# First projection unit of a hybrid attention and RWKV-7 block cut into three column parts

## What is computed

```python
h = jnp.concatenate([meta, x], axis=1)               # 528 x 1024
u = rms_norm(h, norm_mix_pre[l]) @ w_in[l]           # 528 x 5376
u_sb, u_rw, gate_sb, gate_rw = jnp.split(u, cut, axis=-1)
o_sb = stick_breaking_attention(sq, sk, sv)
o_rw = rwkv7_time_mix(...)
merged = sigmoid(gate_sb) * (o_sb @ w_branch_sb) + sigmoid(gate_rw) * (o_rw @ w_branch_rw)
h = h + rms_norm(merged @ w_out[l], norm_mix_post[l])
f = (silu(f @ w_ffn_gate) * (f @ w_ffn_up)) @ w_ffn_down    # f = rms_norm(h)
h = h + rms_norm(f, norm_ffn_post[l])
```

## Time and profile before

| | |
|---|---|
| median of 3 runs | 890.42 us (890.24 to 892.93) |
| the profiled execution, its own time | 892.45 us |
| its span, first to last instruction | 890.6 us |
| busy: PE / PEld | 98% / 81% |
| busy: DVE / ACT / POOL | 55% / 46% / 10% |
| the chain that ended last: PE / DVE / issue, ACT | 93% / 5% / 1% each |
| moved by the transfers | 82.82 MB, 93 GB/s over the span |

### The profile page before, as it was taken

How to read it: one execution, slowest core, us unless ns; L and a number is a source line. 1 busy time by engine, 2 the same in 40 slices (tenths; PEclk the granted TensorE clock), 3 DMA queues, 4 the chain that set the end, 5 groups by cost and what they waited for, 6 DMA issues and landing times.

```text
span 890.6 us, 19075 instructions
## 1 busy us (share of the span) xinstructions
PE 874.9 (98%) x8261; PEld 724.3 (81%) x8261; DVE 487.5 (55%) x644; ACT 412.6 (46%) x573; POOL 92.4 (10%) x92
## 2 busy tenths in 40 slices
PE   6999999999999999999999999999999999999997
PEld 5999999867787777767888898888888888888886
DVE  5459997346767656639575754444444444422333
ACT  6444666359788765555343642222222222211331
POOL 2015543111010101041100000000000000000000
PEclk9999999999999999999999999999999999999999
DMA  9322223311201121142267323333333333333321
GB/s 276 101 83 85 71 72 96 119 50 38 73 4 39 39 74 38 38 131 72 87 221 269 85 67 100 94 94 94 94 94 94 94 94 94 95 96 96 103 85 71
DMA packets 109008, 82.82 MB, mean 93 GB/s; under 512 B 2895, under 2 KB 99449, under 8 KB 108682
## 3 DMA queue, kind: packets, MB, share of 16 engines
q1 hardware_dynamic: 108938, 81.77, 30.3%
HBM read 75.99 MB, written 5.77 MB: 92 GB/s over the span
## 4 chain that ended last, share of the span: by engine, by line
PE 93%; DVE 5%; issue 1%; ACT 1%; DMA 0%; DVEq 0%; SPq 0%
PE psum L576 47%; PE psum L1850 18%; PE psum L1601 9%; PE psum L1638 6%; PE psum L1775 2%; PE psum L1893 2%; PE psum L1494 2%; PE psum L1785 1%; DVE w_lo L566 1%; PE psum L1756 1%; PE psum L1804 1%; DVE shift_diff L1168 1%; PE psum L1485 1%; DVE k_mod L1209 1%; DVE v_t L1173 1%
## 5 line engine op out<-in xcount | busy, mean ns | idle before, releaser
L576 PE MATMUL psum<-h_hi,w_hi 128*128 128x512 f32 (+1 forms) x736 | 230.7, 349 | 0.8 <-DVE w_lo L566 0.8
L576 PE MATMUL psum<-h_lo,w_hi 128*128 128x512 f32 (+1 forms) x736 | 229.7, 347 | 0.0
L576 PE MATMUL psum<-h_hi,w_lo 128*128 128x512 f32 (+1 forms) x736 | 228.7, 346 | 0.0
L566 DVE TENSOR_TENSOR w_lo<-w_raw,w_hi 128x1024 fp32r<-128x1024 f32 x69 | 88.3, 1280 | 113.3 <-ACT w_hi L561 109.0
L576 PEld LDWEIGHTS psum<-h_hi,w_hi 128*128 128x128 f32 x736 | 127.8, 188 | 22.3 <-issue 1.9
L576 PEld LDWEIGHTS psum<-h_lo,w_hi 128*128 128x128 f32 x736 | 127.7, 188 | 18.5 <-issue 0.5
L576 PEld LDWEIGHTS psum<-h_hi,w_lo 128*128 128x128 f32 x736 | 127.8, 188 | 17.7
L1080 ACT ACTIVATE w_hi<-w_raw 128x1024 fp32r<-128x1024 f32 x44 | 46.7, 1062 | 171.6 <-PE psum L576 164.4
L1440 DVE TENSOR_TENSOR w_lo<-w_raw,w_hi 128x1024 fp32r<-128x1024 f32 x44 | 53.9, 1226 | 130.6 <-ACT w_hi L1080 126.4
L561 ACT ACTIVATE w_hi<-w_raw 128x1024 fp32r<-128x1024 f32 x70 | 73.8, 1056 | 77.2 <-PE psum L1850 55.8
L1850 PE MATMUL psum<-w_hi,act_hi 128*128 128x512 f32 x144 | 45.7, 390 | 0.0
(11 more groups left out here) (304 smaller groups left out, 1538.0 us busy)
## 6 DMA issues: line engine op xcount, KB each, us to landing
w_raw<-in_w_in SPq DMA_DIRECT2D x42, 512.0 KB, 4.0
w_raw<-in_w_g SPq DMA_DIRECT2D x22, 512.0 KB, 3.8
w_raw<-in_w_u SPq DMA_DIRECT2D x22, 512.0 KB, 3.9
w_raw<-in_w_d SPq DMA_DIRECT2D x22, 512.0 KB, 3.5
w_raw<-in_w_out SPq DMA_DIRECT2D x8, 512.0 KB, 5.2
kept_gates<-gate_raw SPq DMA_DIRECT2D x10, 256.0 KB, 2.9
sig_t<-kept_gates SPq DMA_DIRECT2D x10, 256.0 KB, 3.0
x_in<-in_x SPq DMA_DIRECT2D x4, 512.0 KB, 7.3
```

The costliest lines, as they stand in the source:

```text
L566: nc.vector.tensor_sub(lo[:], raw[u % RAW][:], hi[:].bitcast(F32)).then_inc(w_split, 1)
L576: mm = nc.tensor.matmul(o, w[:, (w0 + i) * P:(w0 + i + 1) * P], xs[:, k, c0:c1], start=(n == 0), stop=(n == total - 1))
```

## The change

Unit 0's first half is no longer one part of 264 columns but two, columns 0 to 143 (meta and block 0) and columns 144 to 263; with columns 264 to 527, untouched, that makes three. The first part waits for block 0 alone. ScalarE rounds block 0 before it squares block 2's input. The subtraction that makes `w_lo` of unit 0 is shared: VectorE does columns 0 to 511 (the first four feature slices, new semaphore `w_first`), GpSimd columns 512 to 1023 (`w_split` as before). VectorE makes the rest of block 0 ahead of `mean(3)`. The transposes of block 2 now stand after the whole of both parts.

```diff
--- before.py
+++ after.py
@@ -478,6 +478,7 @@
         v_out = sem("v_out")
         prep_pe, prep_act, prep_dve, prep_pool = (sem(f"prep_{e}") for e in ("pe", "act", "dve", "pool"))
         blk_ok = sem("blk_ok")
+        w_first = sem("w_first")
         ones_ok = sem("ones_ok")
         gain_pe = sem("gain_pe")
         gain_ok = sem("gain_ok")
@@ -518,6 +519,8 @@
 
             if u >= RAW:
                 sp.wait_ge(w_split, u - RAW + 1)
+            if u == RAW:
+                sp.wait_ge(w_first, 1)
             if u < U_MIX:
                 sp.dma_start(raw3(u), tile_of(w_in, ORDER[u][1])).then_inc(w_in_raw[u % RAW], 16)
             elif u < U_OUT:
@@ -677,13 +680,8 @@
         def _(pool):
             g = nc.gpsimd
 
-            def lo_beside(us):
-
-                for u in us:
-                    pool.wait_ge(w_hi_done, u + 1)
-                    g.tensor_sub(w_lo[u % SPL][:], raw[u % RAW][:], w_hi[u % SPL][:].bitcast(F32)).then_inc(w_split, 1)
-
-            lo_beside([0])
+            pool.wait_ge(w_hi_done, 1)
+            g.tensor_sub(w_lo[0][:, 512:1024], raw[0][:, 512:1024], w_hi[0][:, 512:1024].bitcast(F32)).then_inc(w_split, 1)
             pool.wait_ge(const_in, 16 * 5)
             g.tensor_copy(bytes_[:], masks_f[:]).then_inc(edge, 1)
             for t in stage:
@@ -821,8 +819,8 @@
             block_hi(0)
             root(2)
             hi_unit(act, 0)
+            block_hi(1)
             square(3)
-            block_hi(1)
             root(3)
             block_hi(2)
             hi_unit(act, 1)
@@ -1137,8 +1135,10 @@
             mean(2)
             block_lo(0)
             scale(2)
+            dve.wait_ge(w_hi_done, 1)
+            v_.tensor_sub(w_lo[0][:, 0:512], raw[0][:, 0:512], w_hi[0][:, 0:512].bitcast(F32)).then_inc(w_first, 1)
+            block_lo(1)
             mean(3)
-            block_lo(1)
             block_lo(2)
             scale(3)
             mean(4)
@@ -1507,13 +1507,18 @@
             pe.wait_ge(ident_in, 16)
             for i in range(3):
                 block_transpose(i)
+            near = META + P
+            pe.wait_ge(w_first, 1)
+            pe.wait_ge(n_lo, 3)
+            unit_part(0, range(0, 4), psum[:, 0, 0:near], 0, near)
             pe.wait_ge(w_split, 1)
+            pe.wait_ge(n_lo, 4)
+            unit_part(0, range(4, KT), psum[:, 0, 0:near], 0, near)
             pe.wait_ge(n_lo, 5)
-            unit_part(0, range(0, 4), bank(0, HALF), 0, HALF)
+            unit_part(0, range(0, 4), psum[:, 0, near:HALF], near, HALF)
             pe.wait_ge(n_lo, 6)
-            unit_part(0, range(4, 5), bank(0, HALF), 0, HALF)
+            unit_part(0, range(4, KT), psum[:, 0, near:HALF], near, HALF)
             block_transpose(3)
-            unit_part(0, range(5, KT), bank(0, HALF), 0, HALF)
             block_transpose(4)
             pe.wait_ge(w_split, 2)
             unit_part(1, range(KT), bank(2, HALF), 0, HALF)
```

## The result

The changed kernel takes 897.09 us (median of 20 runs, 894.02 to 903.21), the kernel before 891.76 us beside it (20 runs, 890.12 to 893.28). The ratio is 1.0078, with a 95% interval of 1.0063 to 1.0093: slower by 0.8%. The forecast was 891.3 with a range up to 893.9, and no change as the likeliest case. It was wrong.

What follows compares the result with a forecast made beforehand. TensorE, busy 874.9 of 890.6 us, was taken as the bound. Opening: 14.0 + 5.33 + 1.74 + 2.89 + 2.04 = 26.0 us against 25.12, +0.9 us on the median 890.42, giving 891.3 us; range 889.4 to 893.9.

Steps and rivals of the forecast that it cites:

- Whatever moves the moment at which TensorE reaches the fixed sequence behind the opening moves the end by the same amount: TensorE after 25 us: its longest wait groups are 0.8 us each, so an opening's gain or loss reaches the end unchanged.
- I take the distance of before: 4.07 us after the first matmul of unit 0: TensorE's opening: the pace rises from slow to fast at 18.1 us; each slow microsecond costs half a microsecond.
- +0.9 us: End of the opening: the small transpose comes at 26.0 us against 25.12, and the whole time grows equally.
- early rival: Opening: pace rises at 16.3, no change (890.4); second form, counted from 10.44, 0.9 us faster (889.5). Chance 0.15.
- slow rival: Unit 0: 48 narrow matmuls and 16 transposes stay slow, pace rises 4.07 us into unit 1; +7.3 us, 897.7. Chance 0.17.
- The start of unit 0 (earlier by 1.4 us): Opening: first matmul of unit 0 at 14.0 instead of 15.42 us, held last by block 1's transposes.
- half of a 1.22 us subtraction ends at 12.8: VectorE, unit 0's weight rest: its half starts after block 1's scaling at 12.19 and is done at 12.8 us.
- the price of a narrow matmul: Unit 0 on TensorE: 0.111 us each at the fast pace, 0.213 us at the slow, hardly shrinking with columns.
- The added work: Unit 0 on TensorE: 48 narrow matmuls (5.33 us) replace 24 wide ones (2.89 us), +2.44 us; heading says 2.2.
- its last rival: Opening: TensorE starts no earlier, at 15.4, and the added work stays; +2.3 us, 892.7. Chance 0.05.
- The work pushed back: ScalarE and VectorE behind the opening: later roundings, scaling and unit 1's rest (20.9 instead of 20.0) stay covered.
- The upper bound: Top of the forecast range: 893.9 us, said to be the forecast's upper end (+1.7 us) with the 2.7 us spread.

Runs made afterwards that it cites:

- padded kernels: Kernel before plus 24, then 8, unread 16x16 matmuls ahead of the first transposes: 895.37 us (1.0042) and 896.03 us (1.0042).
- light load: Changed kernel with the weight load issued at 292.0 us cut from 512 to 64 KB: 896.41 us (1.0058).
- run with borders put back: Changed kernel plus 52 tiny matmuls (208 instructions), leaving the stream one short of a whole block longer than before's: 893.51 us (1.0038).
- run without GpSimd's half: Changed kernel with the second half of unit 0's rest moved from GpSimd to VectorE, behind block 0's; unit 0 starts at 13.67, small transpose at 24.66 us.
- late profiles: Profiles with all 48 narrow matmuls slow: kernel before with only unit 0's first half split (903.3 us), and the changed kernel's execution of 902.70 us.
- dummy transposes and filler: Dummy transposes plus tiny matmuls that nearly restore the block borders: on the kernel before 890.98 us (0.9988), on the changed kernel 892.88 us (1.0009).
- dummy transposes alone: Changed kernel with eight dummy transposes, four ahead of the first transposes and four ahead of unit 0, no tiny matmuls: 897.54 us (1.0053).

## Why the prediction was wrong

**"Whatever moves the moment at which TensorE reaches the fixed sequence behind the opening moves the end by the same amount"** is the first step that failed. The sequence is fixed, but where its blocks of instructions are cut is not: 49 more instructions ahead moved every border, and one of them from wide products into 64 x 64 ones. Price: 2.5 us more of stop (3.0 against 0.5), and in some executions 3.4 or 6.8 us at the lower clock, which cost 1.3 to 2.1 us and 2.4 to 2.7 us more. No rival named it. Shown by the padded kernels, the light load and the run with borders put back.

**"I take the distance of before: 4.07 us after the first matmul of unit 0"** is the second. One profile of the kernel before had the rise at 19.5, and I made it a rule; that kernel's own times already stand in two groups some 2 us apart, and an early rise gives 1.5 us of it (small transpose 23.6 instead of 25.1); with dummy transposes the upper group is gone. Three times were shown then, two at 890.3 and one at 892.9, and I took them for spread. In the five profiles of the change the rise comes either by 14.8 or not until 28.9; the forecast's 18.1 is in none, so that its +0.9 us had the direction right by luck. The early rival priced the first course, in its second form (rise at 14.5, -0.9 us): -0.3 measured against the profiled run of before, and the 0.6 us between them is the later start of unit 0. Against a run of before whose pace also rises early it is +1.3. The slow rival, "the narrow matmuls don't bring the rise", priced the second: 48 slow narrow ones and slow transposes, +7.3 us forecast, +6.5 measured (31.59 against 25.12). It had 0.17 and came in nine of twenty. Only its last step was off: the rise came 0.7 us into unit 1, not 4.07. I had argued from 16 transposes that brought no rise in one execution that transposes don't bring it. The Trainium skill says so too, "TensorE: Matmul & The Clock Gate", section "PE-mode transpose": it doesn't count as busy the same way. The traces here speak against it. In the run without GpSimd's half the pace rose at 13.4, when TensorE had done nothing but transposes since 9.38, behind 2.68 us of idleness. In the late profiles it rose one to three wide matmuls behind 16 unbroken transposes (29.4 and 28.9), in the kernel before 4.07 us behind the first wide one. With dummy transposes and filler, and nothing but transposes from 8.4 and 8.1 us on, it rose at 14.6 and 13.95.

**"The start of unit 0 (earlier by 1.4 us)"** was mis-sized: 0.8. The term "half of a 1.22 us subtraction ends at 12.8" left out that GpSimd makes its half at the same time, until 13.34; VectorE's ended at 13.88, 0.54 us behind that, about its own length. Shown by the run without GpSimd's half (0.61 us, from start to start). The Trainium skill has the rule, "SBUF — State Buffer", section "Who interferes with whom": a VectorE instruction with two SBUF inputs contends with a GpSimd instruction that reads SBUF, and the later one blocks until the first is done. The trace agrees, 1.76 us against 0.61. The rests of the blocks, whose one input is in PSUM, took 0.62 us each in the earlier trace rows, the first ones beside GpSimd's 2.51 us, so those rows could not show it.

**Right**: the price of a narrow matmul, 0.111 forecast, 0.112 measured at the fast pace, and 0.213 forecast, (24.88 - 14.62) / 48 = 0.214 measured at the slow one. The formula of the Trainium skill that the prediction set against it, in the section "Back-to-back issue gap", would have given about half at the fast pace; that section means it for isolated matmuls, and its figure for a stream of loads and matmuls, about 81 ns at 128 columns, is below the measured 0.112 us too. The added work is 48 x 0.112 - 24 x 0.1205 = 2.5 us; the prediction's working has 2.44, while its heading says 2.2 and its last rival 2.3. The work pushed back stayed hidden, but barely: unit 1's rest stood at 20.40 and ended at 21.6 instead of 20.9, and unit 1 began at 21.71, without a wait.

**The upper bound** of the range doesn't follow from its terms: 890.42 + 1.6 and a spread of 2.7 us give 894.7, not 893.9. The measured 897.09 lies outside of both.

**The sum without the two surprises** can be read from the runs with transposes and borders held: 23.54 to 25.07 at the small transpose, +1.5 us, where my terms with the measured start give -0.8 + 2.44 = +1.6. The medians are 890.98 and 892.88, +1.9; the last 0.4 us arises behind the opening and was not traced further. So even at its best the change doesn't pay: 24 extra matmuls cost more than the earlier start gives.

## What to carry over

Splitting a matmul's columns where the price is per instruction buys an earlier start at a known rate; it must be weighed against all of the instructions it adds, and an instruction costs not only its own time but moves every later border of the code. Where a kernel has stretches of very short products, look for stops with the releaser "issue" and note at which instruction number they stand, before and after; filler that restores the count tells in one run whether a loss is of this kind. And read the single times of a kernel before taking one profile's course as its rule: two groups can mean that some event is left to chance. Here filling holes with harmless transposes took the upper group away in 28 executions of three kernels.

## What was not expected of the hardware

- TensorE's instructions arrive over DMA in blocks of 16 KB, 256 of them. Near 300 us a fetch begins 0.7 to 1.1 us behind the crossing of a border in the kernel before and the change, 2.1 to 2.9 us behind it, over all profiles, where 768 KB of data have just been issued, and 0.8 us at the same border with the light load. It lasts some 1 us there, and the instructions are taken up 1.2 to 1.5 us after it has landed. A block of 64 x 64 products lasts 2.0 us, less than that chain.
- The moment of the first rise of the pace differs between executions of one program: 13.9 to 14.8 us in four profiles of the change, 28.9 in the fifth. In three profiles (28.6, 28.9 and 29.4) 48 narrow products ran for over 10 us at the slow pace without a break and without a rise; with the dummy transposes alone they began at the slow pace too, and it rose 1.7 us into them, at 16.4. What decides it in an execution stays open; no run here tells it.
- The granted clock's column stays at 1.00 through an opening in which every spacing is double.
- After a stop of 3 us the clock fell in some executions and not in others (3.09 and 3.28 us without a fall, 3.00, 3.09 and 3.12 with one, of the change alone; in other kernels 2.31, 2.59, 2.70 and 3.00 us with one, 2.71 and 3.10 us without).
- A 16 x 16 product in fp32 is four instructions in the stream.
